# Finishing a scan turn's group norm inside the next turn, and summing its squares on VectorE

## What is computed

```python
xbc, conv_hist_new = _causal_dwconv(xbc, conv_hist, conv_w)      # four taps
xbc = jax.nn.silu(xbc + conv_b)
xs, Bm, Cm = jnp.split(xbc, [...], axis=-1)
...                                                              # chunked scan gives y
y = jnp.concatenate(ys, axis=1) + xs.astype(f32) * D_skip.astype(f32)[:, None]
u = y.reshape(b, L, SSD_INNER) * jax.nn.silu(z.astype(f32))
ug = u.reshape(b, L, SSD_GROUPS, SSD_INNER // SSD_GROUPS)
ug = ug * lax.rsqrt(jnp.mean(ug * ug, axis=-1, keepdims=True) + EPS)
u = (ug.reshape(b, L, SSD_INNER) * norm_w.astype(f32)).astype(h.dtype)
y_ssd = u @ w_ssd_out
```

## Time and profile before

| | |
|---|---|
| time, median of 3 runs | 1428.02 us (1427.01 to 1428.05) |
| the profiled execution: its own time | 1430.2 us |
| the profiled execution: span from first to last instruction | 1428.5 us |
| mean granted TensorE clock | 0.953 |
| busy PE / PEld / DVE / ACT / POOL | 1324.7 / 1027.3 / 567.5 / 377.9 / 457.0 us |
| pe_block's matmuls (L584), h_parts | 3840, 551.5 us busy, mean 305 ns recorded, overlapping |
| chain that ended last, by engine | PE 75%, DVE 12%, issue 4%, ACT 3%, DMA 3% |

### The profile page before, as it was taken

One profiled execution on the slowest core, in us unless ns is written; L12 is line 12 of the kernel. 1 busy time (PEld: TensorE's weight loads), 2 busy tenths in 40 slices (PEclk: granted clock), 3 DMA queues, 4 the chain that ended last, 5 costly groups with the idle time before them and its releaser, 6 DMA issues.

```text
span 1428.5 us, 23149 instructions
## 1 busy us (share of the span) xinstructions
PE 1324.7 (93%) x9087; PEld 1027.3 (72%) x9087; DVE 567.5 (40%) x816; ACT 377.9 (26%) x574; POOL 457.0 (32%) x380
## 2 busy tenths in 40 slices
PE   4999999999989999998999999999987999999990
PEld 4999999999759877975987799994474444444430
DVE  5444441026566754955676550011153111111115
ACT  4212124344234324333342531210121111101102
POOL 5444432345333533533252454330002112122110
PEclk8999999999989999999999999999956999999995
DMA  5223222235107303520631222337612999999925
GB/s 144 75 75 87 74 68 65 78 84 151 48 13 186 109 0 110 132 65 7 182 104 43 81 74 75 89 104 267 279 49 67 363 368 374 370 360 376 378 97 203
DMA packets 179334, 209.75 MB, mean 147 GB/s; under 512 B 12988, under 2 KB 154428, under 8 KB 170896
## 3 DMA queue, kind: packets, MB, share of 16 engines
q1 hardware_dynamic: 167970, 187.97, 40.2%
q10 hardware_dynamic: 4134, 11.11, 2.2%
q0 software_dynamic: 7168, 9.81, 1.9%
HBM read 196.93 MB, written 32.34 MB: 160 GB/s over the span
## 4 chain that ended last, share of the span: by engine, by line
PE 75%; DVE 12%; issue 4%; ACT 3%; DMA 3%; SPq 1%; DVEq 1%; ACTq 0%; POOLq 0%; POOL 0%
PE acc L584 36%; PE pT L944 8%; PE acc L819 5%; PE pS L957 4%; PE acc L983 4%; DVE area L1149 4%; PE pY L747 2%; PE pS L991 2%; PE pS L691 2%; DMA ring<-in_w_in 1%; PE acc L920 1%; PE acc L713 1%; DVE big L1220 1%; PE pY L927 1%; PE pS L753 1%
## 5 line engine op out<-in xcount | busy, mean ns | idle before, releaser
L584 PE MATMUL acc<-h_parts,ring_parts 128*128 128x328 f32 (+1 forms) x3840 | 551.5, 305 | 12.6 <-DVE h_parts L1047 6.9
L584 PEld LDWEIGHTS acc<-h_parts,ring_parts 128*128 128x128 f32 x3840 | 537.7, 192 | 29.0 <-issue 28.2
L1736 POOL TENSOR_TENSOR ring_parts<-ring,ring_parts 128x1024 fp32r<-128x1024 f32 x104 | 263.2, 2531 | 419.3 <-ACT ring_parts L1468 419.3
L1468 ACT ACTIVATE ring_parts<-ring 128x1024 fp32r<-128x1024 f32 x104 | 110.0, 1058 | 371.1 <-PE acc L584 353.6
L944 PE MATMUL pT<-area,big 128*64 128x512 f32 x384 | 116.1, 611 | 0.2 <-ACT big L1665 0.2
L584 PE MATMUL acc<-u_parts,ring_parts 128*128 128x264 f32 (+1 forms) x640 | 109.4, 299 | 0.0
L584 PEld LDWEIGHTS acc<-u_parts,ring_parts 128*128 128x128 f32 x640 | 96.4, 188 | 0.0
L1149 DVE SCALAR_TENSOR_TENSOR area<-area,xvec 128x616 f32<-128x616 f32 x72 | 90.1, 1252 | 10.5 <-DVE area L1147 0.6
L944 PEld LDWEIGHTS pT<-area,big 128*64 128x64 f32 x384 | 35.5, 140 | 78.8 <-issue 78.8
L584 PE MATMUL acc<-area_parts,ring_parts 128*128 128x264 f32 (+1 forms) x512 | 91.1, 299 | 0.0
L584 PEld LDWEIGHTS acc<-area_parts,ring_parts 128*128 128x128 f32 x512 | 78.4, 188 | 0.0
(11 more groups left out here) (332 smaller groups left out, 1708.5 us busy)
## 6 DMA issues: line engine op xcount, KB each, us to landing
ring<-in_w_in SPq DMA_DIRECT2D x80, 512.0 KB, 4.1
area<-in_w_gate SPq DMA_DIRECT2D x24, 1024.0 KB, 6.3
area<-in_w_up SPq DMA_DIRECT2D x24, 1024.0 KB, 9.3
area<-in_w_down SPq DMA_DIRECT2D x24, 1024.0 KB, 11.5
area<-in_state_ssm SPq DMA_DIRECT2D x16, 512.0 KB, 7.0
out<-area SPq DMA_DIRECT2D x16, 512.0 KB, 5.3
ring<-in_w_ssd_out SPq DMA_DIRECT2D x16, 512.0 KB, 4.2
ring<-in_w_gate SPq DMA_DIRECT2D x8, 1024.0 KB, 11.5
```

The lines of the kernel that those rows point to most:

```text
L584: m = nc.tensor.matmul(acc[a][:, h, 0:n], w[s][:, k, :], x[:, k, h * HALF:h * HALF + n], start=first and k == 0 and w is w_hi and x is hi, ...
L1468: a_.activation(w_hi[b % 2], w_raw[b % 2], ACT.Copy).then_inc(hi_done, 1)
L1736: gp.tensor_tensor(w_lo[b % 2], w_raw[b % 2], w_hi[b % 2].bitcast(F32), ALU.subtract).then_inc(lo_done, 1)
```

## The change

Two things are done at once. First, DVE adds up the four tiles of squares (two adds, of 1184 and 592 elements), and TensorE then multiplies one tile a half in place of four; it waits for the second add by `s_sq`, which now counts two a turn. Second, the reciprocal and the scaling of turn g (`norm_end`) move in DVE's program to turn g + 1, behind convolution 1 and ahead of convolution 2, together with the load of `dg`. Turn 0 is written out ahead of the loop, and the last turn's `norm_end` behind it.

```diff
-                pe.wait_ge(s_sq, g + 1)
+                pe.wait_ge(s_sq, 2 * g + 2)
                 for h, pb in ((0, pT), (1, pS)):
                     n = HALF if h == 0 else T - HALF
-                    for k in range(GK):
-                        m = nc.tensor.matmul(pb[:, 0:n], ones[:, :], sq[:, k, h * HALF:h * HALF + n],
-                                             start=k == 0, stop=k == GK - 1)
+                    m = nc.tensor.matmul(pb[:, 0:n], ones[:, :], sq[:, 0, h * HALF:h * HALF + n], start=True, stop=True)
                 m.then_inc(p_gn, 1)
...
-            with dve.Fori(0, GROUPS) as g:
-                link = chain(dve, dve_chain, start, g, 25)
-                link(v.tensor_copy(dg[:, :, :], dnv[:, bass.ds(g * GK, GK), :]))
+            def norm_end(g, link):
+                dve.wait_ge(s_rm, g + 2)
+                link(v.reciprocal(rms, rms))
+                for k in range(GK):
+                    u_k = uT[:, bass.ds(g * GK + k, 1), :].rearrange("p a b -> p (a b)")
+                    x = v.scalar_tensor_tensor(u_k, u_k, dg[:, k, 1:2], rms, ALU.mult, ALU.mult)
+                x.then_inc(s_un, 1)
+                dve.wait_ge(s_un, g + 1)
+
+            def scan_turn(g, link, first):
                 v.memset(st, 0.0).then_inc(s_st, 1)
                 for c in range(6):
+                    if c == 2:
+                        if not first:
+                            norm_end(g - 1, link)
+                        link(v.tensor_copy(dg[:, :, :], dnv[:, bass.ds(g * GK, GK), :]))
...
                 v.tensor_tensor(u_g, u_g, sz, ALU.mult).then_inc(s_uz, 1)
-                dve.wait_ge(s_rm, g + 2)
-                link(v.reciprocal(rms, rms))
-                for k in range(GK):
-                    u_k = uT[:, bass.ds(g * GK + k, 1), :].rearrange("p a b -> p (a b)")
-                    x = v.scalar_tensor_tensor(u_k, u_k, dg[:, k, 1:2], rms, ALU.mult, ALU.mult)
-                x.then_inc(s_un, 1)
-                dve.wait_ge(s_un, g + 1)
-                assert link.count[0] == 25, link.count
-            start += GROUPS * 25
+                dve.wait_ge(s_sq, 2 * g + 1)
+                link(v.tensor_tensor(sq[:, 0:2, :], sq[:, 0:2, :], sq[:, 2:4, :], ALU.add))
+                v.tensor_tensor(sq[:, 0, :], sq[:, 0, :], sq[:, 1, :], ALU.add).then_inc(s_sq, 1)
+
+            link = chain(dve, dve_chain, start)
+            scan_turn(0, link, True)
+            start += link.count[0]
+            with dve.Fori(1, GROUPS) as g:
+                link = chain(dve, dve_chain, start - 26, g, 26)
+                scan_turn(g, link, False)
```

More of the change, by code:

```diff
@@ L1215, in _ @@
                 v.tensor_tensor(u_g, u_g, sz, ALU.mult).then_inc(s_uz, 1)
-                dve.wait_ge(s_rm, g + 2)
-                link(v.reciprocal(rms, rms))
-                for k in range(GK):
-                    u_k = uT[:, bass.ds(g * GK + k, 1), :].rearrange("p a b -> p (a b)")
-                    x = v.scalar_tensor_tensor(u_k, u_k, dg[:, k, 1:2], rms, ALU.mult, ALU.mult)
-                x.then_inc(s_un, 1)
-                dve.wait_ge(s_un, g + 1)
-                assert link.count[0] == 25, link.count
-            start += GROUPS * 25
+                dve.wait_ge(s_sq, 2 * g + 1)
[7 more added lines that the diff above has]
+                scan_turn(g, link, False)
+                assert link.count[0] == 26, link.count
+            start += (GROUPS - 1) * 26
+            link = chain(dve, dve_chain, start)
+            norm_end(GROUPS - 1, link)
+            start += link.count[0]
             for c in range(1, 4):
```

## The result

| | before | after |
|---|---|---|
| median, 17 runs each | 1427.92 us | 1432.23 us |
| lowest and highest | 1425.41, 1429.66 | 1428.95, 1435.03 |
| after over before | | 1.0036 [1.0028, 1.0045] |
| the profiled execution: span | 1428.5 us | 1431.4 us |
| busy PE / DVE | 1324.7 / 567.5 us | 1318.8 / 572.2 us |

The change makes the kernel 0.36% slower. The time lies inside of the stated range, but outside of the 0.2% that I held most likely. TensorE has 5.9 us less to do and the kernel takes 4.3 us more.

What follows compares the result with a forecast made beforehand. VectorE's stretch from norm to L678 was taken as the bound at turn boundaries, its start held by block 2's DMA. Three boundaries +3.0 us and last turn -1.3 gave +1.7 on 1428.02: 1429.7 us, range 1424.5 to 1433.5.

Steps and rivals of the forecast that it cites:

- What bounds the stretch: Between norm and L678, VectorE has no slack; TensorE would idle about 3 us ahead of block 6, about 2 ahead of L678.
- Turn 2's sum: Boundary of turns 1 and 2: VectorE's start +2.3, held time about -0.8, clearing -0.4; convolution 3 starts 1.2 us later.
- Behind L678: Chunk parts behind L678: nothing changed there, so the boundaries' shift passes through them.
- The other two boundaries: Ends of the other two turns with a next turn: TensorE leads by 0.2 us more, so +0.9 us each.
- The last turn: No convolutions behind it: the root starts at 814.3 in place of 815.64, -1.3 us lasting to the end.
- The rival of the clock: TensorE's clock falls behind block 10, scaling held in full: each boundary costs 2.1 us, time 1433.0 us; chance 0.15.
- The rival of a shorter stretch: Subtractions fall into VectorE's gaps, each boundary loses 2.0 us per subtraction: time 1423.7 us, floor 1414; chance 0.18.

Runs made afterwards that it cites:

- e3: The changed kernel with reciprocal and scaling ahead of convolution 4 instead of convolution 2: 1432.87 us, ratio to before 1.0028.
- e10: The changed kernel with GpSimd subtracting only a quarter of each weight block of the scan: 1413.02 us, ratio to before 0.9888.
- e1: The kernel before with only the adds and the one-tile norm on TensorE, reciprocal and scaling in their old place: 1427.08 us, ratio 0.9998.
- e2: The kernel before with only reciprocal, scaling and load of `dg` moved behind convolution 1, norm still eight matmuls: 1426.04 us, ratio 0.9993.
- e7: The changed kernel with TensorE's norm matmul of one tile made four times over: 1429.13 us, ratio to before 1.0009.
- e8: The changed kernel with ACT's copy of block 0 ahead of split and root, GpSimd's two histories ahead of its subtraction: 1421.15 us, ratio to before 0.9952.
- e6: The changed kernel with the load of the next turn's block 2 issued earlier by SP: 1417.96 us, ratio to before 0.9936.

## Where the prediction held and where it didn't, step by step

The forecast of 1429.7 us was 2.5 us short, inside of its own range. The kernel is slower for the reason that carried the sum, a stretch of VectorE that starts later and is held twice; the term that was mis-sized is that of the boundaries, +3.0 where +5.1 was measured. That nothing would change in the chunk parts was wrong, and two errors of over 4 us there cancelled, which is luck.

- **What bounds the stretch: right.** The reciprocal is at 579.8 (foretold about 580), convolution 0 starts 0.33 us behind the copy (0.3), convolution 2 is clean, there is no idle time ahead of block 4, 2.60 ahead of block 6 (3.0) and 2.16 ahead of L678 (2.2).
- **Turn 2's sum: right in kind, 0.5 us short.** Behind the copy's end I had 23.67 us to the start of convolution 3, and it is 24.08: convolution 0 took 5.70, not 5.4, convolution 2 took 0.1 more, and there are 0.2 us between reciprocal and scaling that I left out; the gap ahead of convolution 2 is 0.2 shorter than taken. Behind it all is as foretold.
- **Behind L678: put at nothing.** I wrote that nothing is changed there. VectorE's program of turn 0 is, since it is written out now, and the chunk part of that turn is 4.25 us shorter, while those of turns 1 to 3 are 4.4 us longer with a lower clock. Neither stands in the sum.
- **The other two boundaries: the term that was off most.** I gave them +0.9, since TensorE would lead by more there and more of block 5's subtraction would be covered. It can't lead into block 2, which waits for the copy of block 0 at all three boundaries (0.98, 0.96 and 1.01 us). All three have one pattern, the scaling 4.38, 4.36 and 4.38 us. I had the 1.1 to 2.1 us of earlier TensorE in mind without asking which accumulator block 2 writes. With turn 2's sum and its error at all three, +3.0 becomes +5.1.
- **The last turn: half of it came.** The adds were costed well (end 2.24 us behind the squares against 2.35 taken), but the root starts 4.42 us behind the squares, where I had 3.63. The wait for TensorE is gone, as said; what is late next is ACT itself. This is the end of the last turn, ACT:

```profile
818.26 1.06 ACT L1483 ACTIVATE ring_parts<-ring 128x1024 fp32r<-128x1024 f32 x1 [2.04 <-PE acc L584]
819.34 1.28 ACT L1623 ACT_TABLE_LOAD   x1
820.63 0.48 ACT L1623 ACTIVATE area<-pT,eps 128x264 f32<-128x264 f32 x1
```

The split stands ahead of the root in ACT's program and waits for the end of block 10, then come a split and a table load. So -1.3 became -0.5.
- **The rival of the clock (1433.0 us) had the size and not the reason.** Its mechanism was a slower block 1, behind 1.7 us of new idle time, that pushes block 5's subtraction behind the reciprocal. The idle time was 0.60 us, since block 10 took 9.01 us instead of 7.97. Block 1 took 6.97 us for 48 matmuls at the full clock, and the clock was 1.00 from the copy to L678 at this boundary. The lower level came behind the new idle time instead. At the boundaries it costs 0.3 us, in turn 1, where it falls on block 6 (11.26 us for what takes 9.73). In the chunk parts of turns 1 to 3 it holds for 37.4 us where it held for 17.1, and they take 4.4 us more; how much of that the change's own idle time brings, one profile of each kernel can't tell, so this rival isn't excluded as a part of the loss. The Trainium skill, page "TensorE: Matmul & The Clock Gate", Part 1, has throttled as the default state and activity as what releases it. The 10.2 us behind 4.03 us of idle time in e3 agree with it; behind 2.15 to 2.19 us the rows show both levels.
- **The rival of a shorter stretch (1423.7, floor 1414)** was the right one for a kernel whose subtractions are small: e10 is at 1413.0. The kernel before with the same quarter is at 1416.0, so 3.0 us of that are the change's. Here no subtraction fell into a gap.
- **Both halves in one sum.** The terms were costed one after the other, and the sum hid that two of them depend on each other: with the reciprocal behind convolution 1, TensorE should not be earlier. e1, e2 and e7 show it at the boundaries; the profile of before could have, had I moved block 4's subtraction by 1 us either way. That the meeting is the whole of the 5.1 us isn't shown: in e7 1.2 of the 1.7 us at this boundary are gone, and in e2 1.3 are, but at the first boundary only 0.3 and 0.4 of 1.75.

## What to carry to other kernels

Where one engine's steps are held by another's, cost an edit by where the holding steps fall after it, and shift them by a microsecond both ways before trusting the sum: a faster engine off the bound can bring the hold onto a step that minds it. Before counting time saved on the busiest engine, name what its next instruction waits for (an accumulator, a split, a table), and cure that first: the same adds were worth nothing in e1 and 5.6 us behind an earlier load. A slot in which the bound engine idles is worth more than one in which it doesn't, so look first for work that can move into that slot, as convolution 0 does in e8. And compare parts one by one before calling their sum unchanged: here a gain of 4.25 us and a loss of 4.4 looked like nothing.

## What the runs showed of the hardware

- **A step is held by its kind, not by its size.** GpSimd's subtraction (2.4 us) left the reciprocal alone (3.85 us with all of a subtraction under it, in e7). It held a copy of 128 x 8 elements for 2.13 us instead of 0.17, and the first step of a convolution for 2.31 instead of 0.54. In e6 it held an add of 592 elements for 2.79 us instead of 0.78. I had held that only steps reading two SBUF operands stand still; the copy and the convolution's first step read one tensor of elements. The convolution's step is quick for its size when free (616 elements in 0.42 to 0.54 us, where a step with two operands takes 0.86). The Trainium skill, page "SBUF — State Buffer", "Who interferes with whom", says that VectorE in a 2-port mode contends with GpSimd, that the one that issues first has the port for its whole instruction and that the other blocks. The two rows agree with it, as both steps end with or just behind the subtraction that had started first; in which mode they ran no row shows.
- **Adding work to the busiest engine made the kernel faster**: 3.0 us more at each norm, 3.1 us less for the whole (e7).
- **The lower clock level can come behind idle time of 2 us, and need not.** Ahead of L678 2.16 us brought 3.4 us of it in the changed kernel, and 2.15 to 2.19 us brought none in e2 and e8; 4.03 us brought 10.2 in e3. Before, behind 0.88 us, there was none at this place.
- **The lower level cost some 0.3 us for each microsecond in the chunk parts**: 74.80 us with 3.4 us of it, 77.76 with 13.6, in one execution of the kernel before.
